# Spatial gate's layer norm: the eight tiles are added up on GpSimd before TensorE sums them, and the steps of the gate are spread over more blocks

## What is computed

```python
z = h @ w_in[l] + b_in[l]
z_u, z_v, z_h, z_g = jnp.split(z, split_pts, axis=-1)
y_a = spatial_gating(gelu(z_u), gelu(z_v), sgu_ln_g[l], sgu_ln_b[l], sgu_w[l], sgu_b[l]) @ w_branch_a[l]
...
def spatial_gating(u, v, ln_g, ln_b, w_s, b_s):
    vn = layer_norm(v, ln_g, ln_b).reshape(bsz, n_chunks, SGU_CHUNK, SGU_GROUPS, SGU_GROUP_DIM)
    mixed = jnp.einsum('gqp,bnpgc->bnqgc', w_s, vn) + b_s.T[None, None, :, :, None]
    return u * mixed.reshape(bsz, s, SGU_WIDTH)
```

## Time and profile before

| what | value |
|---|---|
| runs | 2765.8, 2762.38, 2761.29 us, median 2762.38 us |
| profiled execution | 2759.44 us, of it 2757.7 us span |
| TensorE matmul busy | 2574.7 us, 93% of the span |
| VectorE busy | 2009.0 us, 73% |
| ScalarE busy | 1389.8 us, 50% |
| GpSimd busy | 772.8 us, 28% |
| TensorE's granted clock, mean | 0.971 of full |

### The profile page before, as it was taken

The page is one execution under the profiler, slowest core; times in us unless marked ns, Lnnn a source line. Parts: engine busy times, 40 slices in busy tenths (PEclk is TensorE's granted clock), DMA queues, the critical chain, the costliest instruction groups (busy, mean ns, idle before and its releaser), DMA issues.

```text
span 2757.7 us, 42775 instructions
## 1 busy us (share of the span) xinstructions
PE 2574.7 (93%) x16616; PEld 2335.7 (85%) x16616; DVE 2009.0 (73%) x2588; ACT 1389.8 (50%) x2177; POOL 772.8 (28%) x740
## 2 busy tenths in 40 slices
PE   4589998999997999999999979999799999999979
PEld 2478887888985888888888869999689999999978
DVE  6888766778867876545555568888767888888855
ACT  0144433444435444444554457667556666666653
POOL 0200000001213620000111037766203665655530
PEclk9899999999998999999999989999899999999989
DMA  8877755787773876555555534544354444444424
GB/s 312 325 271 270 241 195 168 235 270 249 269 248 107 285 257 231 188 186 182 192 191 190 184 99 163 166 153 153 108 190 161 153 154 153 147 152 148 150 96 160
DMA packets 146339, 534.61 MB, mean 194 GB/s; under 512 B 16631, under 2 KB 16792, under 8 KB 145688
## 3 DMA queue, kind: packets, MB, share of 16 engines
q1 hardware_dynamic: 143176, 520.33, 56.1%
q0 software_dynamic: 2960, 11.54, 1.3%
HBM read 525.51 MB, written 6.29 MB: 193 GB/s over the span
## 4 chain that ended last, share of the span: by engine, by line
PE 71%; DVE 12%; issue 6%; DMA 5%; ACT 4%; POOL 1%; SPq 0%; DVEq 0%; POOLq 0%; ACTq 0%
PE ps L549 28%; PE ps L553 21%; PE ps L551 7%; PE ps L552 7%; DMA ring<-in_w_ada 4%; DVE wl L983 3%; ACT wh L1692 2%; DVE AF L1002 2%; PE ps L594 1%; PE ps L920 1%; PE ps L676 1%; PE ps L821 1%; PE ps L584 1%; POOL misc L2230 1%; PE ps L664 1%
## 5 line engine op out<-in xcount | busy, mean ns | idle before, releaser
L983 DVE TENSOR_TENSOR wl<-ring,wh 128x1024 fp32r<-128x1024 f32 x784 | 1032.5, 1330 | 403.8 <-ACT wh L1692 399.0
L553 PE MATMUL ps<-A,wl 128*128 128x256 f32 x4480 | 1264.5, 282 | 0.0
L1692 ACT CAST wh<-ring 128x1024 fp32r<-128x1024 f32 x784 | 813.4, 1044 | 383.0 <-PE ps L553 375.7
L553 PEld LDWEIGHTS ps<-A,wl 128*128 128x128 f32 x4480 | 857.9, 192 | 0.4
L549 PE MATMUL ps<-A,wh 128*128 128x512 f32 x2176 | 776.3, 401 | 18.6 <-DVE A L987 8.4
L551 PE MATMUL ps<-A,wh 128*128 128x256 f32 x2304 | 674.5, 293 | 14.3 <-DVE A L987 9.7
L549 PE MATMUL ps<-B,wh 128*128 128x512 f32 x1792 | 648.0, 405 | 30.7 <-DVE wl L983 12.9
L552 PE MATMUL ps<-A,wh 128*128 128x256 f32 x2304 | 653.8, 284 | 0.0
L549 PEld LDWEIGHTS ps<-A,wh 128*128 128x128 f32 x2176 | 413.0, 190 | 119.7 <-issue 14.4
L553 PE MATMUL ps<-B,wl 128*128 128x256 f32 x1792 | 508.0, 283 | 0.0
L551 PEld LDWEIGHTS ps<-A,wh 128*128 128x128 f32 x2304 | 443.8, 193 | 17.8 <-issue 10.5
(11 more groups left out here) (246 smaller groups left out, 2292.7 us busy)
## 6 DMA issues: line engine op xcount, KB each, us to landing
ring<-in_w_m SPq DMA_DIRECT2D x256, 512.0 KB, 4.6
ring<-in_hgrn_w_in SPq DMA_DIRECT2D x160, 512.0 KB, 3.8
ring<-in_w_ada SPq DMA_DIRECT2D x144, 512.0 KB, 6.5
ring<-in_w_in SPq DMA_DIRECT2D x144, 512.0 KB, 5.0
ring<-in_conv_w_in SPq DMA_DIRECT2D x96, 512.0 KB, 3.9
AF<-in_w_ada SPq DMA_DIRECT2D x48, 512.0 KB, 8.8
ring<-in_w_ab SPq DMA_DIRECT2D x32, 512.0 KB, 5.1
ring<-in_w_o SPq DMA_DIRECT2D x32, 512.0 KB, 4.9
```

Of the source, the lines that this page charges most:

```text
L553: return e.matmul(dst[:, 0:256], lo, x[:, 0, :], start=False, stop=last)
L983: e.tensor_tensor(low[:], ring[SLOT[h]][:], hi[:].bitcast(F32), ALU.subtract).then_inc(s.lo, 1)
L1692: e.copy(wh[h % NSPLIT][:], ring[SLOT[h]][:]).then_inc(s.hi, 1)
```

## The change

GpSimd adds the eight `v` tiles into `v_sum` (seven additions), and later their squares into `v_squares` (seven more). TensorE sums each of the two over partitions once. The generator steps are drawn apart: TensorE sums the mean at i = 41 and the squares at i = 46, and the groups run from i = 50 to 65; VectorE subtracts four tiles in each of i = 41 and 42 and does the reciprocal at i = 48; ScalarE squares two tiles in each of i = 42 to 45, in which each square from the third on waits for an addition on GpSimd, and takes the root at i = 47. GpSimd's additions are put between its DMA issues.

```diff
@@ buffers
+    v_sum, v_squares = misc[:, 2048:2304], misc[:, 2304:2560]
@@ tensor_program, spatial
-            for i in range(8):
-                w.wait_ge(s.vmu, 1)
-                w.wait_ge(s.vsq, i + 1)
-                row_sum(ps[3][:, 0:256], 1, sgu_sq[i % 2], i, 8, s.vss)
-                if i % 4 == 0:
-                    yield
-            yield
-            yield
-            yield
+            w.wait_ge(s.vsum, 7)
+            w.wait_ge(s.spec, 16)
+            row_sum(ps[3][:, 0:256], 1, v_sum, 0, 1, s.vmean)
+            for _ in range(5):
+                yield
+            w.wait_ge(s.vmu, 1)
+            w.wait_ge(s.vsum, 14)
+            row_sum(ps[3][:, 0:256], 1, v_squares, 0, 1, s.vss)
+            for _ in range(4):
+                yield
@@ tensor_program, main loop
-                    if 34 <= i < 42:
-                        w.wait_ge(s.uv, i - 25)
-                        w.wait_ge(s.spec, 16)
-                        row_sum(ps[3][:, 0:256], 1, vv(i - 34), i - 34, 8, s.vmean)
@@ vector_program, spatial
-                if g % 4 == 0:
+                if g % 4 == 3:
                     yield
-            yield
+            for _ in range(5):
+                yield
...
-            w.wait_ge(s.vss, 8)
+            w.wait_ge(s.vsq, 8)
@@ scalar_program, spatial
-            w.wait_ge(s.vmean, 8)
+            w.wait_ge(s.vmean, 1)
             e.copy(statb[:, 0:256], ps[3][:, 0:256]).then_inc(s.vmu, 1)
             for g in range(8):
+                if g % 2 == 0:
+                    yield
                 w.wait_ge(s.vsub, g + 1)
-                w.wait_ge(s.vss, g - 1)
-                e.activation(sgu_sq[g % 2].rearrange("p (a b) -> p a b", a=1), vv(g).unsqueeze(1),
-                             ACT.Square).then_inc(s.vsq, 1)
-                if g % 4 == 0:
-                    yield
-            w.wait_ge(s.vss, 8)
+                w.wait_ge(s.vsum, 7 + g - 1 if g >= 2 else 0)
+                e.activation(sgu_sq[g % 2], vv(g), ACT.Square).then_inc(s.vsq, 1)
+            yield
+            yield
+            w.wait_ge(s.vss, 1)
@@ gpsimd_program
-        for m in range(7):
+        def sum_v(g):
+            w.wait_ge(s.uv, 9 + g)
+            w.wait_ge(s.vsum, vsum.n)
+            w.wait_ge(s.zh, 24)
+            vsum.up(e.tensor_tensor(v_sum, vv(0) if g == 1 else v_sum, vv(g), ALU.add))
+
+        def sum_squares(g):
+            w.wait_ge(s.vsq, g + 1)
+            w.wait_ge(s.vsum, vsum.n)
+            vsum.up(e.tensor_tensor(v_squares, sgu_sq[0] if g == 1 else v_squares, sgu_sq[g % 2], ALU.add))
+
+        for m in range(5):
             spectrum(m)
+        for g in range(1, 4):
+            sum_v(g)
+        spectrum(5)
+        for g in range(4, 6):
+            sum_v(g)
+        spectrum(6)
+        for g in range(6, 8):
+            sum_v(g)
         group(0)
         spectrum(7)
+        group(1)
         for g in range(1, 8):
+            sum_squares(g)
+        for g in range(2, 8):
             group(g)
```

More of the change, by code:

```diff
@@ L192 @@
     "tr ut fwd hv inv skip y "
-    "vmean vmu vsub vsq vss vn vt vtc vmx vad ug "
+    "vsum vmean vmu vsub vsq vss vn vt vtc vmx vad ug "
     "ablo gy mx gp "
@@ L2205, in group @@
             e.dma_start(bsb[g % 2], d["sgu_b"][g:g + 1, :].to_broadcast([P, P])).then_inc((s.ws0, s.ws1)[g % 2], 16)
-        for m in range(7):
-            spectrum(m)
+        vsum = Tally(s.vsum)
+        def sum_v(g):
[8 more added lines that the diff above has]
+        for m in range(5):
+            spectrum(m)
+        for g in range(1, 4):
[6 more added lines that the diff above has]
+            sum_v(g)
         group(0)
         spectrum(7)
+        group(1)
         for g in range(1, 8):
+            sum_squares(g)
+        for g in range(2, 8):
             group(g)
```

## The result

The changed kernel takes 2744.2 us (median of 4 runs, 2743.86 to 2751.42), the kernel before 2762.24 us (4 runs, 2761.29 to 2765.8). The ratio is 0.9939, with a 95% interval of 0.9919 to 0.9959: 18.0 us faster, where 18.9 and a time of 2743.5 had been forecast. The interval alone allows anything from 11 to 22 us, so the traces have to say how much of the agreement is more than luck. The profiled execution took 2743.86 us.

What follows compares the result with a forecast made beforehand. TensorE bounds the kernel, with a hole of waits at lower clock. 19.15 - 0.43 (mean's row sum) + 0.65 (wait) - 0.43 (second row sum) gives 18.9 us off 2762.38: 2743.5 us, own range 2740 to 2747, 8 in 10 2738 to 2750.

Steps and rivals of the forecast that it cites:

- The bound and the most that can be gained: Four TensorE rounds from 368.94 to 484.49 take 115.55 us against 96.40: 19.15 us too many, the most available.
- Row sums, 6.02 us: 14 of TensorE's 16 row sums go, at 0.43 us each, and are saved in full.
- The waits, 12.27 us, and 0.65 at i = 47: TensorE's 9.1 us waiting for squares, 3.2 us of handoffs at lower clock, and a 0.65 us wait all go.
- The mean at i = 41: GpSimd's last tile additions end between 435.0 and 437.0, before TensorE wants the sum at 438.9: cost nothing.
- The squares in block 43: ScalarE's squares hold the cast; lo(90) done at 13.0 to 15.5 us, wanted at 15.3: stall 0 to 0.2, taken as 0.
- VectorE at i = 48 and 49: Reciprocal and scaling behind a chunk reduction: lo(102) done after 13.7 us, TensorE reaches half 102 after 14.3.
- Contention: GpSimd's additions lengthen VectorE's two-input operations by 7.7 us at most over twelve blocks; on the path 0 to 1 us.
- the rule of the Trainium skill: Two-SBUF-input VectorE and SBUF-reading GpSimd instructions exclude each other; at i = 43 the sum would be 0.9 us smaller.
- The clock: A shift can turn a lower-clock dip, like that behind the reduction at 356 us, on or off: 1.7 us either way.
- the row sums alone: Rival: TensorE gives all waits back elsewhere, only the row sums' 6.0 us are gained: 2756.4 us; chance 0.05.
- the hold: Rival: late casts in blocks 43 to 45, or VectorE at 48 and 49, cost 6 to 9 us; chance 0.14.
- the slow alternation: Rival: alternating squares and additions on two buffers makes it slower, needing additions of some 6 us; 2763 and up; chance 0.03.

Runs made afterwards that it cites:

- apart_only: Changed kernel's steps drawn apart, but GpSimd adds nothing and TensorE still sums sixteen tiles: 2752.37 us, ratio 0.9955 to the kernel before.
- mean_only: Against the kernel before, GpSimd adds only the mean's tiles; squares and their row sums stay as they were: 2759.6 us, ratio 0.9987.
- slow_adds_4: Changed kernel with four idle additions of the same size ahead of each addition of squares: 2765.58 us, ratio 0.9995 to the kernel before.
- slow_adds_2: Changed kernel with two idle additions of the same size ahead of each addition of squares: 2752.13 us, ratio 0.9952 to the kernel before.
- adds_only: GpSimd's additions as in the changed kernel, other engines' steps where the kernel before had them, squares summed at i = 43: 2755.42 us, ratio 0.9974.

## Why the prediction was right, point by point

**The bound and the most that can be gained.** The rounds before held 19.15 us too many, and the changed kernel's four rounds take 97.05 against the 96.83 worked out. Right.

**Row sums, 6.02 us.** apart_only against the changed kernel gives 5.8 us, mean_only 3.0 of its seven (3.4 with a shorter wait). Right, and separable from the waits: the additions gain 5.1 us with the steps at the old places and 5.8 at the new ones.

**The waits, 12.27 us, and 0.65 at i = 47.** 12.9 together; apart_only shows 13.2. Right, though how the 3.2 us that no wait names divide between handoffs and lower clock was not tried. It was the steps that had to move: with the additions alone one wait of 10.2 us took their place.

**The mean at i = 41.** GpSimd's timeline after:

```profile
433.05 0.58 POOL L2198 DMA_DIRECT2D XR<-kscr  x1 [13.65 <-DVE misc L1152]
433.65 2.43 POOL L2214 TENSOR_TENSOR misc<-misc,BF 128x256 f32<-128x256 f32 x2
...
457.68 0.55 POOL L2198 DMA_DIRECT2D XR<-kscr  x1 [20.52 <-DVE misc L1152]
...
459.32 0.75 POOL L2219 TENSOR_TENSOR misc<-misc 128x256 f32<-128x256 f32 x1
460.65 0.73 POOL L2219 TENSOR_TENSOR misc<-misc 128x256 f32<-128x256 f32 x1 [0.59 <-ACT misc L1775]
...
473.15 0.82 POOL L2219 TENSOR_TENSOR misc<-misc 128x256 f32<-128x256 f32 x1 [0.87 <-ACT misc L1775]
```

The two last additions of tiles end at 436.1, within the 435.0 to 437.0 given, ahead of the row sum at 438.82. That the times themselves agree is chance: seven row sums less ahead of this place (3.0 us) and the late start of this execution (3.1 us) cancel. What counts is the distance of 2.7 us. Spectrum 6, behind two additions of tiles, was issued at 433.05 with GpSimd idle for 13.65 us before it, so nothing was late in that queue. The last addition of squares ends at 473.97, 4.6 us ahead of the row sum at 478.54. The prediction had not worked out that distance.

**The squares in block 43.** ScalarE's timeline after, and VectorE's `lo(90)`:

```profile
460.16 0.42 ACT L1775 ACTIVATE misc<-BF 128x256 f32<-128x256 f32 x1 [10.08 <-POOL misc L2219]
461.47 0.42 ACT L1775 ACTIVATE misc<-BF 128x256 f32<-128x256 f32 x1 [0.90 <-POOL misc L2219]
461.80 1.03 ACT L1691 CAST wh<-ring 128x1024 fp32r<-128x1024 f32 x1
```

```profile
462.86 1.23 DVE L981 TENSOR_TENSOR wl<-ring,wh 128x1024 fp32r<-128x1024 f32 x1 [4.75 <-ACT wh L1691]
```

The forward transform started at 450.99, so `lo(90)` ended 13.1 us later, against 13.0 worked out with the short additions. Half 90 starts 2.8 us ahead of the transpose at 469.11, at 466.3, 15.3 us in that count. The spare time of 2.2 us is that of the short additions, as forecast; the stall of up to 0.2 us that the long ones would have given did not come. slow_adds_4 and slow_adds_2 show that beyond the spare time a hold does cost, and that the stretch grows by more than the waits where the clock falls behind them. So the prediction had the place right, and its price for a lost cover, one for one, too low.

**VectorE at i = 48 and 49.** `lo(102)` ended at 508.0, 12.8 us behind the reduction, against 13.7; half 102 started at 509.4, 14.2 us behind it, against 14.3. No wait.

**Contention.** `lo` in the stretch runs 1.22 us in the middle and 2.10 at most, where I took 1.77 as its longest, and two more take 1.76. So the allowance for contention was too small. It cost nothing, as VectorE's idle time covers it. The sum was not touched by the rule of the Trainium skill that I had weighed (SBUF — State Buffer, "Who interferes with whom"): the 0.9 us it would have cost at i = 43 did not come, because VectorE was idle there. Elsewhere the durations come near what it says: beside the two additions from 433.65 on, which took 0.75 and 1.54 us, one `lo` took 0.88 us longer than alone, about the length of an addition. No run tried the rule by itself.

**The clock.** The dip behind the reduction at i = 32 is in both profiles with 5.39 us, so no change of clock at that place joined or left the sum. The allowance of 1.7 us for it was right: with the same gap, other traces have the transform at 3.70 us.

The rivals: the row sums alone would have left 13 us of waits; the hold and the slow alternation exist as mechanisms, and slow_adds_4 shows the price at which the second cancels the gain (a stretch of 139.94 us for 140.50). An addition with its idle ones took 3.5 to 6.1 us there, 4.6 on average, below the 6 us that I had put. The prediction had counted only ScalarE's holds, one for one. It left out TensorE's own wait for the last addition, with 6.7 us the largest of the three, and the lower clock behind the waits.

## What to carry to other kernels

A helper's result that stands in the bottleneck engine's own queue costs the whole chain behind it; move the step that waits to where its result is long ready, and see which queue the wait then stands in and how much work the bottleneck still has in hand there. Price the instructions that go and the waits that go by themselves, and try each alone: here the additions gave 5.1 us at the old places and 5.8 at the new ones, and moving the steps gave 13.2. Fewer row sums did not take the waits away (8.7 of 9.1 us stayed in mean_only, and 10.2 came in adds_only); the moved steps did. Where executions differ by more than the effect, compare one stretch between two marks of the trace (two executions of the changed kernel agree in it within 0.1 us), and test the spare time by making the suspected work dearer.

## What the runs showed of the hardware that I had not expected

A wait of TensorE of under 1 us can bring the lower clock, and need not. With one of 0.66 to 0.76 us ahead of the reduction at i = 32, the transform behind took 5.39 us or more in eight of ten traces and 3.70 at full clock in two (28.68 us for the round with the dip, 26.8 to 26.9 without it, 25.98 and 25.89 without wait or dip). In slow_adds_4, 13.1 us of waits come with 5.4 us more. VectorE's `lo` took 2.10 us, against 1.22 alone, beside two GpSimd additions, which took 2.43 us together:

```profile
433.39 2.10 DVE L981 TENSOR_TENSOR wl<-ring,wh 128x1024 fp32r<-128x1024 f32 x1
```

The start of the stretch wanders by up to 6 us between executions that have nearly the same code before it. Part of that is this dip: the round ahead takes 26.79 to 30.25 us with the gap in place. Most of it is older: the transpose of i = 24 already starts anywhere from 293.3 to 297.8 us in the ten experiments. What makes it wander ahead of that was not tried.
